# Forget gate's logits: tokens instead of heads on the partitions, and the norm's scale applied per partition

## The reference

```python
def shared_kv(x, kv_norm_g, kv_w, kv_f_bias, k_norm_g):
    h = rmsnorm(x, kv_norm_g)
    proj = h @ kv_w
    k = to_heads(proj[..., :D])
    v = to_heads(proj[..., D:2 * D])
    f_logit = (proj[..., 2 * D:] + kv_f_bias).astype(jnp.float32)
    k = rmsnorm(k, k_norm_g)
    log_f = jax.nn.log_sigmoid(f_logit)
    c = jnp.cumsum(jnp.transpose(log_f, (0, 2, 1)), axis=-1)
```

## Time and profile before

| | us |
|---|---|
| median of 3 runs | 1413.74 |
| the runs | 1411.14 to 1414.27 |
| profiled execution, its time | 1413.04 |
| profiled execution, span from first to last instruction | 1411.3 |
| TensorE busy | 1373.9 |
| VectorE busy | 956.9 |
| ScalarE busy | 748.7 |

### The profile page before, as it was taken

The page is one execution under the profiler, slowest core; times in us unless marked ns, Lnnn a source line. Parts: engine busy times, 40 slices in busy tenths (PEclk is TensorE's granted clock), DMA queues, the critical chain, the costliest instruction groups (busy, mean ns, idle before and its releaser), DMA issues.

```text
span 1411.3 us, 23234 instructions
## 1 busy us (share of the span) xinstructions
PE 1373.9 (97%) x9694; PEld 1184.3 (84%) x9694; DVE 956.9 (68%) x1486; ACT 748.7 (53%) x1258; POOL 68.6 (5%) x64
## 2 busy tenths in 40 slices
PE   6999999999999999999999999999999999999998
PEld 6789887888889888888889877878888898788887
DVE  6896877665665776766577544576566697666565
ACT  6873434554546675555463446555455536555453
POOL 0014450000010000000000000000000000000000
PEclk9999999999999999999999999999999999999999
DMA  9420005555555415555565544545555653455551
GB/s 330 149 77 13 23 3 212 202 183 192 196 202 179 143 39 177 181 192 196 184 227 183 205 155 144 178 150 186 202 183 188 210 179 120 150 179 183 203 181 59
DMA packets 35288, 230.64 MB, mean 163 GB/s; under 512 B 4176, under 2 KB 5504, under 8 KB 8560
## 3 DMA queue, kind: packets, MB, share of 16 engines
q1 hardware_dynamic: 33376, 223.43, 45.6%
q0 software_dynamic: 1808, 5.74, 1.2%
HBM read 228.08 MB, written 1.05 MB: 162 GB/s over the span
## 4 chain that ended last, share of the span: by engine, by line
PE 89%; DVE 8%; ACT 2%; issue 1%; DMA 0%; SPq 0%; DVEq 0%; ACTq 0%
PE bank L1807 17%; PE bank L1808 17%; PE bank L1809 17%; PE bank L1932 16%; PE bank L1935 8%; PE bank L2188 2%; PE bank L1764 1%; DVE wlo L979 1%; PE bank L2005 1%; DVE arena L1336 1%; PE bank L2024 1%; DVE arena L1211 0%; DVE raw L1356 0%; DVE arena L1356 0%; PE bank L2361 0%
## 5 line engine op out<-in xcount | busy, mean ns | idle before, releaser
L979 DVE TENSOR_TENSOR wlo<-raw,whi 128x1024 fp32r<-128x1024 f32 (+1 forms) x416 | 498.5, 1217 | 255.1 <-ACT whi L452 250.8
L452 ACT ACTIVATE whi<-raw 128x1024 fp32r<-128x1024 f32 (+1 forms) x416 | 425.5, 1041 | 335.5 <-PE bank L1809 232.3
L1807 PE MATMUL bank<-whi,XHL 128*128 128x512 f32 x872 | 342.2, 392 | 0.0
L1808 PE MATMUL bank<-wlo,XHL 128*128 128x512 f32 x872 | 339.6, 389 | 0.0
L1809 PE MATMUL bank<-whi,XHL 128*128 128x512 f32 x872 | 339.4, 389 | 0.0
L1932 PE MATMUL bank<-XHL,whi 128*128 128x512 f32 x1008 | 316.6, 395 | 0.2
L1935 PEld LDWEIGHTS bank<-XHL,wlo 128*128 128x128 f32 x1008 | 189.3, 188 | 44.5
L1935 PE MATMUL bank<-XHL,wlo 128*128 128x256 f32 x1008 | 198.0, 278 | 0.0
L1809 PEld LDWEIGHTS bank<-whi,XHL 128*128 128x128 f32 x872 | 163.7, 188 | 34.4
L1807 PEld LDWEIGHTS bank<-whi,XHL 128*128 128x128 f32 x872 | 163.7, 188 | 34.3 <-issue 1.7
L1808 PEld LDWEIGHTS bank<-wlo,XHL 128*128 128x128 f32 x872 | 163.8, 188 | 32.6 <-issue 0.5
(11 more groups left out here) (308 smaller groups left out, 1307.0 us busy)
## 6 DMA issues: line engine op xcount, KB each, us to landing
raw<-in_w_mlp SPq DMA_DIRECT2D x128, 1024.0 KB, 4.9
raw<-in_w_rv SPq DMA_DIRECT2D x8, 1024.0 KB, 5.0
raw<-in_w_rg SPq DMA_DIRECT2D x8, 1024.0 KB, 4.9
raw<-in_w_reo SPq DMA_DIRECT2D x8, 1024.0 KB, 4.9
raw<-in_w_k SPq DMA_DIRECT2D x4, 1024.0 KB, 10.0
raw<-in_w_v SPq DMA_DIRECT2D x4, 1024.0 KB, 8.3
raw<-in_w_r SPq DMA_DIRECT2D x4, 1024.0 KB, 4.9
raw<-in_w_rwo SPq DMA_DIRECT2D x4, 1024.0 KB, 5.1
```

The costliest lines, as they stand in the source:

```text
L452: act.activation(high, full, ACT.Copy).then_inc(hi_done, 1)
L979: dve.tensor_tensor(low, full, high, ALU.subtract).then_inc(lo_done, 1)
L1807: pe.matmul(out_, xh[xs], wh[ws], start=start, stop=False)
L1808: pe.matmul(out_, xh[xs], wl[ws], start=False, stop=False)
```

## The change

The two sides of the gate's product change places. A 128x128 block of the activations becomes the stationary side and the 16 columns of weights of a k tile the moving one, in three passes for each of two blocks of tokens, so the result has tokens on 128 partitions and 2 x 16 columns in bank 5. `spread_row` goes. VectorE scales each block by the norm's scale of its token, which now is one value per partition, into `fl`. Two transposes (`forget_turned`, at k tile 6 of the same chunk) bring heads back onto the partitions, in bank 6, and VectorE's bias addition reads them there. The split of unit fv+2 on VectorE moves from behind the absolute value to ahead of the wait for the transposes.

```diff
+        f_scaled, f_turned = sem("f_scaled"), sem("f_turned")
@@ VectorE
             dve.wait_ge(f_prod, 1)
             dve.wait_ge(fox_in, 16 * 3)
-            step(dve.tensor_copy(fc[0:NH, :], psum[5][0:NH, T:2 * T]))
-            step(dve.tensor_tensor(fz[0:NH, :], psum[5][0:NH, 0:T], fc[0:NH, :], ALU.add))
-            step(dve.tensor_tensor(fz[0:NH, :], psum[6][0:NH, 0:T], fz[0:NH, :], ALU.mult))
-            dve.tensor_scalar(fz[0:NH, :], fz[0:NH, :], fbias[0:NH, :], None, ALU.add).then_inc(f_z, 1)
+            for m in range(MT):
+                ins = dve.tensor_scalar(fl[:, m * NH:(m + 1) * NH], psum[5][:, m * NH:(m + 1) * NH],
+                                        norm_rstd[:, m:m + 1], None, ALU.mult)
+            ins.then_inc(f_scaled, 1)
+            lo_upto(U0["fv"] + 3)
+            dve.wait_ge(f_turned, 1)
+            dve.tensor_scalar(fz[0:NH, :], psum[6][0:NH, 0:T], fbias[0:NH, :], None, ALU.add).then_inc(f_z, 1)
             dve.wait_ge(f_z, 1)
             dve.scalar_tensor_tensor(fl[0:NH, :], fz[0:NH, :], -1.0, fz[0:NH, :], ALU.mult, ALU.max)\
                 .then_inc(f_abs, 1)
-            lo_upto(U0["fv"] + 3)
             head_inverses(2)
@@ TensorE
                 for k in range(KT):
                     cols = slice(k * NH, (k + 1) * NH)
-                    pe.matmul(psum[5][0:NH, :], WFH[:, cols], XHL[:, k].rearrange("p h t -> p (h t)"), start=(k == 0),
-                              stop=False)
-                    pe.matmul(psum[5][0:NH, 0:T], WFL[:, cols], XH[:, k], start=False, stop=(k == KT - 1))
-                spread_row(norm_rstd, 6, 0, NH).then_inc(f_prod, 1)
+                    for m in range(MT):
+                        ins = passes(psum[5][:, m * NH:(m + 1) * NH], (XH, XL), (WFH, WFL),
+                                     (slice(None), k, slice(m * P, (m + 1) * P)), (slice(None), cols),
+                                     k == 0 and m == 0, k == KT - 1 and m == 1)
+                ins.then_inc(f_prod, 1)
+
+            def forget_turned():
+
+                pe.wait_ge(f_scaled, 1)
+                for m in range(MT):
+                    ins = pe.transpose(psum[6][0:NH, m * P:(m + 1) * P], fl[:, m * NH:(m + 1) * NH], ident[:, :])
+                ins.then_inc(f_turned, 1)
 
-            chunk("fv", 0, "token", mids=((4, query_sums_and_forget),))
+            chunk("fv", 0, "token", mids=((4, query_sums_and_forget), (6, forget_turned)))
```

## The result

| | before | after |
|---|---|---|
| median of 7 runs each, in turns, us | 1411.14 | 1415.66 |
| lowest to highest | 1408.11 to 1414.27 | 1413.92 to 1420.97 |
| ratio after/before, with its interval | | 1.0037 [1.0023, 1.0052] |
| profiled execution, us | 1413.04 | 1415.66 |
| its span | 1411.3 | 1413.9 |

The changed kernel is slower by more than the 0.2% that a measurement can tell from no change. The page of the changed kernel, busy time by engine and shares of the chain, answers to the earlier trace rows: TensorE has 30 instructions and 3.7 us more.

What follows compares the result with a forecast made beforehand. TensorE bounds the kernel, but at the gate VectorE's chain runs beside it and the later sets the attention's start; TensorE +1.74 +0.3 = +2.0 and VectorE +2.1 give +2.1 us, median 1415.8 us, range 1413.0 to 1420.0.

Steps and rivals of the forecast that it cites:

- The block: Forget gate on TensorE: 48 products at 0.11 us, 5.28 us plus one load, +1.74 us over the old block.
- C: Rival at the gate's block: loads don't overlap (0.19 us) or products take two passes; 1419.6 to 1421.0 us, chance 0.09.
- D: Rival at the gate's block: price goes by columns, about 0.02 us per product; 1411.5 us, chance 0.05.
- The row chosen for the price: Attention value products, 128x128 loads with 64 moving columns: the load sets the pace, 0.11 us each.
- The transposes: Two on TensorE, 12 large multiplications after the block: 0.3 us with a semaphore, no cost from waiting for f_scaled.
- VectorE's chain: From the gate's scalings to the first mask: L1508 starts at 488.45 instead of 486.34, +2.1 us.
- the wait for Ln: VectorE after the reciprocal: waits 0.45 us for ScalarE's Ln, no longer hidden behind the split.
- the wait for the transposes: VectorE ahead of the bias addition: half a microsecond of idling until f_turned.
- the moved split: VectorE's split of unit fv+2, ahead of the wait for f_turned: 482.6 to 484.9, weights ready as early as now.
- Both sides end together: At the attention's start: TensorE's and VectorE's sides both arrive about 2.0 to 2.1 us later, neither absorbing the other.
- the forecast without a clock fall: Whole kernel: end moves by +2.1 us, to a median of 1415.8 us; chance 0.46.
- rival B: Clock falls inside or right behind the gate's block: +1.7 or +3.4 us on top, about 1418.5 us; chance 0.36.

Runs made afterwards that it cites:

- lo_back: Changed kernel with VectorE's split of unit fv+2 put back behind the absolute value; 1419.4 us, ratio 1.0055.
- before_lo_ahead: Kernel before, with only VectorE's split of unit fv+2 moved ahead of the wait for the gate's products; 1411.11 us, ratio 1.0000.
- before_fused2: Kernel before with high and low weights as one stationary side and the fv+2 split ahead of the wait, measured a second time; 1408.54 us, ratio 0.9985.
- shared32: Changed kernel with high and low weights side by side as 32 moving columns, 32 loads instead of 48; 1412.3 us, ratio 1.0013.
- split24: Changed kernel with its 48 products in two blocks of 24, at k tiles 2 and 4; 1415.53 us, ratio 1.0034.
- four16: Changed kernel with the block done four times over, 192 loads with 16 moving columns; 1451.31 us in one execution.
- four128: Changed kernel with the block done four times over and the 16 columns repeated to 128, 192 loads; 1427.54 us in one execution.
- spread12: Changed kernel with its 48 products in four blocks of 12, at k tiles 1 to 4; 1413.68 us, ratio 1.0022.

## Why the prediction came out as it did

| from the head sums to the attention | us over before | of it the clock | the rest |
|---|---|---|---|
| changed kernel | 3.81 | 1.70 | 2.11 |
| changed kernel again | 7.03 | 5.12 | 1.91 |
| 128 columns | 2.22 | 0 | 2.22 |
| 32 loads | 2.02 | 1.71 | 0.31 |
| 32 loads, repeated columns | 0.44 | 0 | 0.44 |
| split put back | 8.63 | 5.12 | 3.51 |
| before, fewer columns and split ahead | -1.00 | 0 | -1.00 |
| before, split ahead | -0.06 | 0 | -0.06 |

**The block: right.** Forecast 5.28 us and one load, measured 5.36 from the first product to the large one; 0.112 per product, one pass. Rivals C (0.19, or two passes) and D (0.02) fall with that row. (D's 0.02 is loose: by columns alone, 16 of 512 in 0.23 us are 0.007.) The row chosen for the price, an attention load with 64 columns, was the right one: 16, 32 and 128 columns cost the same.

**The transposes: right in kind, a little high.** 0.22 us instead of 0.3, with no wait for f_scaled.

**VectorE's chain: right.** The clean +2.1 us at the attention is the forecast's sum; the wait for Ln is 0.55 us instead of 0.45, the wait for the transposes 0.39 instead of 0.5 where the clock held, and the moved split is worth 1.4 to 1.6 us at the attention, by lo_back.

**Both sides end together: right.** before_lo_ahead gains 0.06 us from VectorE's side alone; before_fused2, which eases both, gains 1.00.

**The clock: the step that failed.** The prediction put the forecast without a clock fall at 0.46 and rival B at 0.36, and gave the forecast's time. B is what happened: in all six profiled executions with a whole block of few columns or half of it (changed kernel twice, lo_back, shared32, split24, four16) the clock fell at the block, and in none of the others. The prediction named the right doubt, few columns or idling, and then weighed the attention's 1.00 as evidence against B, though its value products move 64 columns for each load of 0.11 us, its other products more, and the new ones 16. four16 and four128 answer it: the clock fell at 16 columns and held at 128, with the engine shown busy in both. The Trainium skill ("TensorE: Matmul & The Clock Gate", Part 1) says that the clock follows how busy the engine has been; the rows here show that a row of busy time without gaps (36.50 of 36.50 us in four16, at 0.50) does not tell on which side of that a stream falls. B's price was also too narrow: 1.7 or 3.4 us were foreseen from the earlier trace rows, and two of the traces lost 5.1; in both the fall came inside the block, so that its own rest ran slow.

**The number itself is right partly by luck.** 1415.8 us was forecast and 1415.66 measured, but the forecast stood on 1413.74, the median of three runs; over seven runs the kernel before has 1411.14. The change measured is thus +4.5 us between the medians (+5.2 by the ratio, with 3.2 to 7.3 as its interval), not +2.1: the forecast's 2.1 and B's 1.7 to 5.1 on top, from execution to execution. The range held both.

**What scatters the runs.** Three other places, all with transposes behind a norm like those of the earlier trace rows, lose the clock in some executions and not in others. Half of the time at the lower level, in us, by place:

| | gate, 480 | 935 | 1117 | 1230 |
|---|---|---|---|---|
| before | 0 | 1.7 | 0 | 3.4 |
| changed | 1.7 | 0 | 1.7 | 1.7 |
| changed again | 5.1 | 3.4 | 3.4 | 1.7 |
| 128 columns | 0 | 1.7 | 3.4 | 1.7 |
| split24 | 1.7 | 0 | 0 | 0 |
| spread12 | 0 | 0 | 0 | 0 |
| 32 loads | 1.7 | 0 | 0 | 3.4 |
| before, split ahead | 0 | 1.7 | 0 | 0 |
| 32 loads, repeated columns | 0 | 0 | 1.7 | 1.7 |
| split put back | 5.1 | 1.7 | 3.4 | 1.7 |
| before, fewer columns and split ahead | 0 | 0 | 0 | 0 |

The changed kernel's row at 1117 is this one:

```profile
1117.00:1120.00 3.00, 3.00 (x16) 3.00 (x15) 3.00 (x7) 3.00 (x8) 0.22 (x1) 0.50 0.71 243
```

Without these losses the spans are 1406.2 us before, 1408.8 and 1407.7 for the changed kernel, 1408.4 with 128 columns and 1405.9 with 32 loads: +1.5 to +2.6 for the change, about what the stretch at the gate shows. split24's is 1409.6 and spread12's 1409.5, a microsecond more than their stretch at the gate accounts for; lo_back's is 1408.7, so its 1.4 us at the attention can't be found in its span. Whether later work adds or gives back this microsecond, or the rest of the trace scatters by as much, stays open: the eleven executions of the kernel before at a mean clock of 0.999 span 1406.1 to 1407.9 us. Why the clock fell behind split24's first block and not behind its second, and why the three other places lose it in some executions only, is open too.

## What to carry to other kernels

When a product's cost is set by the load of its stationary side, put the wide operand on the moving side, or count loads: 48 loads of 128x128 cost 5.36 us here, and leaving out a third of them gave back 1.8 us. Before putting a run of products with very few columns into a stream of large ones, look at the granted clock behind it, not at the busy share; repeating the columns up to what the load hides, or cutting the run into four pieces between large products, kept the clock here at no cost that the times show (two pieces did not keep it). And where two engines' chains end together, cost both: easing one of them gained 0.06 us, easing both 1.0 us.

## What the runs showed of the hardware

- The clock fell from 2.4 to 1.2 GHz with TensorE busy without a gap, on products with 16 moving columns, and held on the same loads with 128 (four16, 36.5 us at 0.50; four128, 23.5 us at 1.00).
- A product with a new 128x128 load costs 0.112 us at the higher clock whether 16, 32 or 128 columns move (changed kernel, shared32, four128), and 0.213 us at the lower clock with 16 (four16).
- This data type, the reduced float32, takes one pass per product with 16 moving columns too (changed kernel, 48 products in 5.36 us); the trace before showed nothing under 256.
